# Gate's last units, post-norm, addition and the next block's first four tiles by token halves; memory tiles freed by ScalarE

## What is computed

```python
        h = rms_norm(x, norm_ffn_pre[i])
        ff = (jax.nn.silu(h @ w_ffn_gate[i]) * (h @ w_ffn_up[i])) @ w_ffn_down[i]
        x = x + rms_norm(ff, norm_ffn_post[i])
        e = (p[i] @ w_ple_proj[i]) * jax.nn.sigmoid(x @ w_ple_gate[i])
        x = x + rms_norm(e, norm_ple[i])
    # the next layer, or the second block, starts with
        h = rms_norm(x, norm_mix_pre[i])
        z = h @ w_in[i]
        o_b = fourier_mix(h)
```

## Time and profile before

| | us |
|---|---|
| median of 3 runs | 2791.32 |
| range of the runs | 2787.62 to 2794.15 |
| the profiled execution | 2788.51 |
| its span in the trace | 2786.7 |
| TensorE busy in it | 2686.7 (96%) |
| VectorE, ScalarE, POOL busy | 1399.1, 1118.8, 411.1 |
| mean granted TensorE clock | 0.992 of full speed |

### The profile page before, as it was taken

The page is one execution under the profiler, slowest core; times in us unless marked ns, Lnnn a source line. Parts: engine busy times, 40 slices in busy tenths (PEclk is TensorE's granted clock), DMA queues, the critical chain, the costliest instruction groups (busy, mean ns, idle before and its releaser), DMA issues. The chain is left out here.

```text
span 2786.7 us, 34822 instructions
## 1 busy us (share of the span) xinstructions
PE 2686.7 (96%) x13520; PEld 2175.8 (78%) x13520; DVE 1399.1 (50%) x2072; ACT 1118.8 (40%) x1759; POOL 411.1 (15%) x320
## 2 busy tenths in 40 slices
PE   7999999999999899999999999999898999899997
PEld 6876778888887787677888888777687688788886
DVE  6665544533324665654453332475588536533423
ACT  6445533422324544654342222453534535522221
POOL 5100002211103310000221110231101012311101
PEclk9999999999999999999999999999999999999999
DMA  4320123132332232012313233222232222122232
GB/s 155 125 86 31 46 77 120 62 104 90 106 106 91 84 121 91 31 46 76 121 61 105 91 106 106 91 76 76 77 120 76 68 99 76 46 96 99 90 108 89
DMA packets 37501, 245.76 MB, mean 88 GB/s; under 512 B 4608, under 2 KB 5632, under 8 KB 8448
## 3 DMA queue, kind: packets, MB, share of 16 engines
q1 hardware_dynamic: 33632, 239.09, 24.8%
q10 hardware_dynamic: 3744, 4.94, 0.5%
HBM read 241.91 MB, written 2.10 MB: 88 GB/s over the span
## 5 line engine op out<-in xcount | busy, mean ns | idle before, releaser
L566 PE MATMUL bank<-h_hi,w_hi 128*128 128x512 f32 x1928 | 764.5, 397 | 7.8 <-DVEq L1596 4.3
L568 PE MATMUL bank<-h_hi,w_lo 128*128 128x512 f32 x1928 | 752.8, 390 | 0.0
L567 PE MATMUL bank<-h_lo,w_hi 128*128 128x512 f32 x1928 | 752.6, 390 | 0.0
L1558 DVE TENSOR_TENSOR w_lo<-raw,w_hi 128x2048 fp32r<-128x2048 f32 x133 | 308.3, 2321 | 350.1 <-ACT w_hi L1083 349.2
L566 PEld LDWEIGHTS bank<-h_hi,w_hi 128*128 128x128 f32 x1928 | 362.5, 188 | 93.7 <-issue 17.5
L568 PEld LDWEIGHTS bank<-h_hi,w_lo 128*128 128x128 f32 x1928 | 362.6, 188 | 76.9
L567 PEld LDWEIGHTS bank<-h_lo,w_hi 128*128 128x128 f32 x1928 | 363.0, 188 | 73.1 <-issue 1.4
L1083 ACT ACTIVATE w_hi<-raw 128x2048 fp32r<-128x2048 f32 x151 | 287.8, 1910 | 243.0 <-PE bank L568 233.5
L1570 DVE TENSOR_TENSOR w_lo<-raw,w_hi 128x2048 fp32r<-128x2048 f32 x60 | 137.6, 2293 | 156.1 <-ACT w_hi L1298 156.1
L566 PE MATMUL bank<-a_hi,w_hi 128*128 128x512 f32 x528 | 205.7, 390 | 0.0
L567 PE MATMUL bank<-a_lo,w_hi 128*128 128x512 f32 x528 | 205.7, 390 | 0.0
(11 more groups left out here) (422 smaller groups left out, 4577.2 us busy)
## 6 DMA issues: line engine op xcount, KB each, us to landing
raw<-in_stream SPq DMA_DIRECT2D x226, 1024.0 KB, 4.8
x<-in_xT SPq DMA_DIRECT2D x4, 512.0 KB, 8.8
out_T<-x ACTq DMA_DIRECT2D x8, 256.0 KB, 2.1
p_f<-in_pT ACTq DMA_DIRECT2D x2, 512.0 KB, 4.0
memf<-in_memT ACTq DMA_DIRECT2D x1, 1024.0 KB, 5.1
cst_sb<-in_cst ACTq DMA_DIRECT2D x1, 409.0 KB, 7.5
pos_i<-in_pos ACTq DMA_DIRECT2D x1, 258.0 KB, 6.3
g_in<-in_gains ACTq DMA_DIRECT2D x3, 4.0 KB, 1.6
```

The lines of the kernel that those rows point to most:

```text
L566: nc.tensor.matmul(ps, wh, xh, start=start, stop=False)
L567: nc.tensor.matmul(ps, wh, xl, start=False, stop=False)
L568: return nc.tensor.matmul(ps, wl, xh, start=False, stop=stop)
L1558: nc.vector.tensor_tensor(lo[:, :], raw[v % 2][:, :], hi[:, :].bitcast(F32), ALU.subtract).then_inc(lo_ready, 1)
```

## The change

**The gate by halves.** `ple` makes its tiles 0 to 3 as before. The last four are made by token halves: 256 tokens from the units 2 and 3, then the other 256 from the units 3 and 2. One bank then holds two feature blocks of one half, side by side. Squares, sum, root, post-norm, addition, high and low part are done in halves too. The first half's sum of squares stands within the second half's matmuls; the second half's sum stands within `begin`.

**The next tiles by halves.** `begin` makes its four tiles in the same manner: the first half from unit 0 and unit 1, the second from unit 1 and unit 0. The early buffer `second` now holds unit 0. The norm's root is made by halves also, and at the kernel's start x comes in eight DMAs of 256 KB in place of four of 512 KB, with the second unit's DMA between the halves.

**The order on the other engines.** ScalarE takes the first half's first four high parts, splits unit 3, takes the other four, and only then the sigmoids of the second half. POOL adds the eight blocks of the first half to x before it adds the second half's squares. In `norm_begun` ScalarE now splits the next two units behind the first and the second half's root.

**Memory tiles.** ScalarE itself releases the bank of `mk` and `mv`; VectorE's part is gone.

```diff
 HALVED = {
     "wout": [2, 4, 7, 8],
+    "ple": [2, 4, 8, 7],
+    "z1a": [0, 3],
...
-            (1, "z1a"): [None, second],
-            (2, "z2"): [None, second],
+            (1, "z1a"): [second, None],
+            (2, "z2"): [second, None],
...
+        def in_turn(half):
+            return (0, 1) if half == 0 else (1, 0)
...
-            def begin(c, st):
+            def begin(c, st, ending=None):
...
+                for half in range(2):
+                    at = cols(half)
+                    for turn, p in enumerate(in_turn(half)):
+                        if half == 0:
+                            pe.wait_ge(lo_ready, c.at("U", st, p + 1))
+                        ps = free_bank(c, st, 2 * half + turn)
+                        hi, lo = home(c, u0 + p)
+                        for k in range(KD):
+                            if turn == 0:
+                                pe.wait_ge(raw_split, c.begun("W", KD * half + k + 1))
+                            for g in range(2):
+                                b = slice((8 * g + k) * P, (8 * g + k + 1) * P)
+                                mm = mac_at(ps[:, cols(g)], hi[:, b], lo[:, b], raw_x_hi[:, k, at], raw_x_lo[:, k, at],
+                                            k == 0 and g == 0, k == KD - 1 and g == 1)
+                            if (half, p, k) == (0, 0, 3) and ending is not None:
+                                half_sum(ending, "ple", 1)
+                            if half == 1 and k == 1:
+                                if turn == 0:
+                                    pe.wait_ge(cst_loaded, 16)
+                                for j in range(2):
+                                    square_sum(sq_tree, c.begun("Q", turn + 1), sq_x[:, j, cols(turn)], j == 0, j == 1, ps=HALF_SS[turn])
+                        mm.then_inc(tile_done, 1)
...
-                    together=0)
-                project_sum(c, "ple", sq_ready, "SQ")
-                pe.sem_inc(tile_done, NO_TILES)
+                    last=4, together=0)
+                last_units(c, "ple", lambda k, at: h_hi[:, k, at], lambda k, at: h_lo[:, k, at], 6)
...
+                ple_gate(4)
+                split_unit(c, "ple", 2)
+                ple_squares(4)
+                ple_gate(5)
                 log_table()
-                root("ple", c, 2, S, D)
+                ple_squares(5)
+                half_root(c, "ple", 0, 3, HALF_RSTD[0][:, 0:HALF])
                 act.wait_ge(gain_loaded, L * 16 + 32)
                 for m in range(KD):
-                    begin_hi(m, (x_ready, c.at("X", "post3", m + 1)))
+                    begin_hi(m, 0, (x_ready, c.at("X", "post3", m + 1)))
+                    if m == 3:
+                        split_unit(c, "ple", 3)
+                for n in (6, 7):
+                    ple_gate(n)
+                for n in (6, 7):
+                    ple_squares(n)
+                log_table()
+                half_root(c, "ple", 1, 6, HALF_RSTD[1][:, 0:HALF])
...
-                        if half == 0 and m == 4:
-                            half_squares(c, st, 1)
+                        if half == 0 and m == (7 if st == "ple" else 4):
+                            half_squares(c, st, 1, ready, kind)
```

More of the change, by code:

```diff
@@ L145, in releases @@
         out.append(("T", n + 1) if done else ("PU", parts))
+    if name == "z2":
+        out[0:2] = [("T", 0), ("T", 3)]
     return out
@@ L161, in stage @@
         c["PU"] = sum(kind == "PU" for kind, _ in rel)
-        c["T"] = {"four1": 16, "four2": 5, "z1b": 4, "ple": KD + NO_TILES}.get(name) or len(TILES[name])
+        c["T"] = {"four1": 16, "four2": 5, "z1b": 4, "uq": 16 + NO_TILES}.get(name) or len(TILES[name])
     c["A"] = A
@@ L788, in project, with last_units @@
                 run(c, st, lambda n, j: (hi(j, slice(0, S)), lo(j, slice(0, S)), need(j) if n == 0 else None), last=4)
+                last_units(c, st, hi, lo, 1)
+            def last_units(c, st, hi, lo, sums_at):
                 u0, seen = c.base[st]["U"], TILES[st][3][-1] // BLK
                 for half in range(2):
-                    for two in range(2):
-                        ps = free_bank(c, st, 4 + 2 * half + two)
+                    for turn, two in enumerate(in_turn(half) if st == "ple" else (0, 1)):
+                        ps = free_bank(c, st, 4 + 2 * half + turn)
                         for i in range(2):
@@ L800, in project @@
                                          i == 0 and j == 0, i == 1 and j == len(t) - 1)
[L801 removed]
+                                if half == 1 and turn == 0 and i == 0 and j == sums_at:
                                     half_sum(c, st, 0)
@@ L1049, in unit_steps @@
                 for n, end in enumerate(ends):
-                    if st in SPLIT_AHEAD and n == len(ends) - 1 and end == u:
-                        split(u)
                     if end == u:
                         evac(n)
-                if u < max(ends) or st not in SPLIT_LATER and st not in SPLIT_AHEAD:
+                if u < max(ends) or st not in SPLIT_LATER:
                     split(u)
@@ L1426, in first_block @@
+                for m in range(KD):
+                    begin_hi(m, 1, (x_ready, c.at("X", "post3", KD + m + 1)))
+                    if m % 2 == 1:
+                        begin_squares(m // 2, 1)
                 assert chain["n"] <= CHAIN_PER_LAYER
@@ L1872, in first_low @@
                 nc.vector.tensor_tensor(lo[:, :], raw[v][:, :], hi[:, :].bitcast(F32), ALU.subtract).then_inc(lo_ready, 1)
-            first_low(0, w_hi[0], w_lo[0])
-            for m in range(KD):
-                begin_lo(m, m + 1)
-            first_low(1, *second)
-            add_begun(KD)
+            first_low(0, *second)
+            for half in range(2):
+                for m in range(KD):
+                    begin_lo(m, half, KD * half + m + 1)
+                    if half == 1 and m == 2:
+                        add_begun(0, 4)
+                if half == 0:
+                    first_low(1, w_hi[1], w_lo[1])
+            add_begun(1, 8)
             start_steps = chain["n"]
@@ L2002, in first_block @@
-                post(c, "ple", "post3", 1, "ple", e, lo=lambda m: begin_lo(m, c.at("W", "begin", m + 1)))
-                add_begun(c.at("SQ", "begin", KD))
+                    if n < 4:
+                        part, by = e[:, n, :], sg[:, n % 2, :]
+                    else:
+                        half = (n - 4) // 2
+                        two = in_turn(half)[n % 2]
+                        part = e[:, 4 + 2 * two:6 + 2 * two, cols(half)]
+                        by = res[:, n - 4, :].rearrange("p (i s) -> p i s", i=2)
@@ new lines, in gate_ple @@
+                    nc.vector.tensor_tensor(part, part, by, ALU.mult).then_inc(tile_free, 1)
+                for n in range(4):
+                    gate_ple(n)
+                    if n % 2 == 1:
+                        split_unit(c, "ple", n // 2)
+                gate_ple(4)
+                split_unit(c, "ple", 2)
+                gate_ple(5)
+                for half in range(2):
+                    at = cols(half)
+                    dve.wait_ge(rms_ready, c.at("N", "post3", half + 1))
+                    for m in range(KD + 2):
+                        if m < KD:
+                            if m >= 2:
+                                dve.wait_ge(x_ready, c.at("X", "post3", KD * half + m - 1))
+                            nc.vector.scalar_tensor_tensor(out=sg[:, m % 2, at], in0=e[:, m, at], scalar=vv("ple", m),
+                                                           in1=HALF_RSTD[half][:, 0:HALF], op0=ALU.mult, op1=ALU.mult).then_inc(post_ready, 1)
+                        if half == 0 and m == 5:
+                            split_unit(c, "ple", 3)
+                        elif half == 1 and m == 2:
+                            add_begun(0, c.at("SQ", "begin", 4))
+                        if m >= 2:
+                            begin_lo(m - 2, half, c.at("W", "begin", KD * half + m - 1))
+                    for n in (6, 7) if half == 0 else ():
+                        gate_ple(n)
```

196 lines of the change are left out of this document (104 added, 92 removed).

## The result

The changed kernel takes **2807.37 us** in the median of 5 runs (2806.61 to 2812.03), against 2791.32 before: the ratio is 1.0057, with a 95% interval of 1.0045 to 1.0068. Timed again beside the experiments (the kernel called after_again), it stood at 1.0067 (1.0053 to 1.0081). So it is slower by 16 us, where the forecast was 8.9 slower. The direction was right, and so was the chain up to the gate's second sum; the size was too small by almost a half, and the measured time stands 0.4 us above the end of the range. The profiled execution of the changed kernel took 2806.61, 18.1 more than that of the kernel before.

The account below looks back on a forecast made before the run. TensorE, busy 96% of the span, was taken to bound the kernel. Seam 1 4.3, seam 2 4.4, start 0.9, memory -0.7 gave +8.9 on 2791.32: 2800.2 us, range 2786 to 2807.

Parts of the forecast that it names:

- The waits of `raw_x_lo` go, and one at the sum takes their place: At each seam: 6.67 us of waiting goes, 6.8 comes at the second half's sum in begin; +2.7 a seam overall.
- The wait for unit 3: In ple's last four tiles: TensorE waits 0.65 us for unit 3's low part, shifting all that follows.
- The clock behind the wait: Behind the wait at the second half's sum in begin: the clock falls again, costing the same 2.0 us.
- The halving: Two half matmuls cost 0.0133 us more than one whole: 2.6 us a seam, 1.3 at the start.
- The norm behind `begin`: Behind begin at each seam: TensorE waits for h_lo; +1.6 us at seam 1, +1.7 at seam 2, from below 0 to 3.
- The start: At the kernel's start: halving +1.3 us, first matmul somewhat earlier; +0.9 taken, from -0.5 to +2.
- Memory tiles: At the memory tiles: between 0 and 2.7 us of VectorE's waiting for its sequencer comes back; -0.7 taken.
- The short wait: Rival, at the second half's sum: unit 3's split hides, wait 2.9 us, clock still falls; 2791.6 us, chance 0.16.
- the other side: Rival, same place: short wait below the clock's falling point (2.18 to 3.13 us), norm free; 2783.7 us, chance 0.12.
- The dearer table load: Rival, sigmoid table load at each seam: costs more than 1.28 us; 2802.8 or 2803.0 us, chance 0.13 with late transfer.
- The hidden norm: Rival, norm behind begin: its waits are hidden as other work slips; 2796.9 us, chance 0.11.

Follow-up runs that it names:

- gates_in_gap: The changed kernel with the second half's two sigmoids taken behind the sixth high part of the first half instead of the eighth; 2803.00 us, ratio 1.0041.
- sum_later: The changed kernel with the gate's second sum of squares behind the eighth block of begin's first turn instead of the fourth; 2803.49 us, ratio 1.0044.
- halved_only: The kernel before with only the matmuls of ple's last four tiles and all of begin issued as two of 256 columns; 2794.24 us, ratio 1.0011.
- all_moved: The changed kernel with ScalarE's second norm split ahead of the second root, second-half sigmoids behind the sixth high part, gate's second sum four blocks later; 2796.52 us.
- mem_alone: The kernel before with only the memory tiles' edit: ScalarE frees the banks of mk and mv, VectorE's pass-on is gone; 2790.41 us, ratio 1.0003.
- all_moved_2: all_moved, but ScalarE's second norm split goes behind the first two h_hi, and VectorE's part behind the first four results and the tiles; 2797.20 us.

## Why the prediction was right or wrong

**The waits of `raw_x_lo` go, and one at the sum takes their place: right.** 6.31 for a forecast of 6.8, with the split of unit 3 ahead of the seventh `sg`, the table load, the sigmoids and POOL's additions in that order. gates_in_gap and sum_later took 2.4 and 2.8 us off it, at the place named. The sum came 34.5 us into the seam for 34.4 forecast, which is partly luck: the last high part was 0.6 late, and POOL's pair took 1.58 where 1.97 was assumed. `begin` still ended 59.8 us into the seam where 59.1 was forecast, 3.5 more than before for 2.7. TensorE's restarts behind the sums and waits, 0.1 to 0.2 each, weren't in the forecast.

**The wait for unit 3: right**, 0.61 for 0.65. **The clock behind the wait: right**, 0.50 in the first four us.

**The halving: right in the changed kernel.** The pace of 0.120 holds there for all but some six half matmuls of `begin`, so the halving cost what was charged, 2.6 a seam, within 0.1. The 1.8 that halved_only shows is less mainly because its slow stretch covers less of the work.

**The norm behind `begin`: the step that failed.** The prediction had 1.1 for block 0 and 0.9 for block 1, less 0.4, which makes 1.6 and 1.7, and no cost of clock. Measured are 2.27, then a granted clock of 0.55, in all 3.6 to 3.7 a seam, which is above the term's upper bound of 3 too. Two things are wrong. POOL's `h_lo` was priced at its 1.27 from the earlier trace rows, a row in which VectorE does other work; in the new order VectorE's subtraction of a unit begins just before it, and it takes 2.86. VectorE's part of that split isn't in the prediction's chain for the norm at all. And no slow clock was counted behind the wait. With the wait of 1.1 that would have been right, as the 1.07 in all_moved shows. But the rivals take, one wait of 2.18 without a fall, for the lower end of the point from which the clock falls. The kernel before has a wait of 2.21 with a fall, at another place, as this row of its stretches shows:

```profile
2013.20:2017.20 4.00, 3.96 (x12) 3.17 (x13) 3.90 (x5) 2.10 (x3) 0.00 (x0) 0.68 0.00 0
```

This term is 2.0 us too small at either seam, some 4 us of the 7 between forecast and result.

**The start, mis-sized as well**: 2.8 for 0.9, above its bound of 2. The first matmul comes 0.4 earlier, but `begin` takes 1.9 longer, where halving was to cost 1.3, and behind it stands the same wait of 2.27 for `h_lo`, with the same 2.86 of POOL beside VectorE's subtraction. The prediction said that this wait is there in either kernel; the kernel before has 1.37 for `cq` in its place. That is another 1.9 of the miss, and the rest of `begin` at the seams is 1.4. These sums are of one profile of each kernel; the start's experiment is halved_only alone. **Memory tiles**: not told from 0 or from -0.7, by mem_alone.

**The rivals.** The short wait and the other side did not come: the splits do hold up `sg`. The dearer table load didn't either, as the sigmoid started 1.30 behind the load's start. The Trainium skill ("ScalarE: Activation LUTs", section "What ACT_TABLE_LOAD costs") states a drain of about 1380 ns besides; these rows show none, ahead of the load or behind it. The hidden norm was the contrary of what happened.

## What to carry to other kernels

Splitting the last tiles so that the chain behind them starts earlier makes the chain's first half early and its second half late: look for what the second half's sum waits for, and how much time TensorE has left behind the last sum, which halving also cuts (from the start of the norm's last sum to where TensorE wants the next stage's first block, 8.6 us before and 5.3 here). Where the chain's engines already have a split of a unit to do in that time, each place tried for it here moved the wait to another item; count the whole queue of the fullest engine between two points, not the one item in the way.

An instruction's duration holds for the neighbours it was measured with. Before pricing a moved POOL instruction, look at what VectorE runs beside it in the new order.

The offset between two profiles grows and shrinks by waits of single executions too, 0.9 us at 478 here. Compare a third profile before putting a term's size down to such a difference.

## What the runs showed of the hardware

- POOL's subtraction of 512 columns takes 1.26 to 1.32 us alone, 2.86 to 3.34 us when a VectorE subtraction of 2048 columns on SBUF operands was running or held up as it started, and VectorE's takes 3.06 in place of 2.29 when POOL's started first.
- The same wait of TensorE doesn't always bring the low clock. Two executions of the same instructions, up to there unchanged, had 2.18 and 2.19 us of waiting at one place. In the kernel before the granted clock behind it was 1.00; in mem_alone it was 0.59, as the row below shows. In all_moved_2 the waits for `h_lo` at the two seams, 1.71 and 1.66, had 0.65 and 1.00 behind them. So the length of the wait alone doesn't decide it.

```profile
1987.20:1991.20 4.00, 4.00 (x11) 3.23 (x12) 1.81 (x3) 2.99 (x5) 0.00 (x0) 0.59 0.76 266
```

- At the low clock, two matmuls of 256 columns take as long as one of 512 (0.213 twice, 0.427); at the full clock they take 0.013 us more.
